# An FFN, attention and FFN layer on eight cores: other chunk split, residual update over two PSUM banks, final scale on one engine, weights cast by the DMA

## The reference

```
x += 1/2 swiglu(rmsnorm(x), w_ffn1_in, w_ffn1_out)      # (silu(g) * u) @ w_out
h  = rmsnorm(x);  q, k, v, forget gates = h @ w_in
o  = concat(8 forgetting-attention heads, 4 differential-attention heads)
x += o @ w_out
x += 1/2 swiglu(rmsnorm(x), w_ffn2_in, w_ffn2_out)
y  = rmsnorm(x)
outputs: y, new k, v and log forget gates, for prompt (2048 rows) and samples (4 x 32 rows a core)
```

## Time and profile before

| | |
|---|---|
| median of 3 runs | 1653.27 us (1652.67 to 1654.9) |
| profiled execution | 1653.27 us, span of its slowest core 1651.5 us |
| spans of the 8 cores | 1642.0 to 1651.5 us, granted TensorE clock 0.988 to 0.991 |
| PE / DVE / ACT / POOL busy | 95% / 44% / 42% / 15% of the span |
| chain that ended last | 83% PE, 5% issue, 4% ACT, 3% DVE, 2% DMA |
| DMA | 137.62 MB; POOL's queue 74.93 MB in 27.3% of 16 engines' span, SP's 60.51 MB in 10.6% |

### The profile page before, as it was taken

One profiled execution on the slowest core, in us unless ns is written; L12 is line 12 of the kernel. 1 busy time (PEld: TensorE's weight loads), 2 busy tenths in 40 slices (PEclk: granted clock), 3 DMA queues, 4 the chain that ended last, 5 costly groups with the idle time before them and its releaser, 6 DMA issues.

```text
span 1651.5 us, 34146 instructions; the slowest of 8 cores (1642.0 to 1651.5 us)
## 1 busy us (share of the span) xinstructions
PE 1562.6 (95%) x11654; PEld 856.6 (52%) x11654; DVE 727.8 (44%) x1489; ACT 690.0 (42%) x1402; POOL 246.1 (15%) x440
## 2 busy tenths in 40 slices
PE   5999999999997998999999999999999999999985
PEld 2544444444443576666766666544544444444431
DVE  4425224325236476666754444454234225234156
ACT  4510110110125576777789999964110110110134
POOL 3200000000013323232321121111000000000035
PEclk9999999999998999999999999999999999999998
DMA  9360131220217547656557555441620320320014
GB/s 288 81 108 14 28 62 21 44 40 14 52 28 207 167 96 135 129 114 125 104 114 138 119 121 121 90 129 52 117 37 0 71 39 1 59 38 2 13 56 161
DMA packets 41642, 137.62 MB, mean 83 GB/s; under 512 B 5121, under 2 KB 7809, under 8 KB 39810
## 3 DMA queue, kind: packets, MB, share of 16 engines
q0 software_dynamic: 17856, 74.93, 27.3%
q1 hardware_dynamic: 23618, 60.51, 10.6%
HBM read 174.63 MB, written 35.72 MB: 127 GB/s over the span
## 4 chain that ended last, share of the span: by engine, by line
PE 83%; issue 5%; ACT 4%; DVE 3%; DMA 2%; POOL 1%; SPq 0%; ACTq 0%; DVEq 0%; POOLq 0%
PE ps L161 82%; PE ps L171 1%; DMA xspill<-s_x 1%; DMA s_x<-xin 1%; DVE s_x L206 1%; DVE s_hn_68 L206 1%; ACT s_P_113 L190 1%; ACT s_junk L190 1%; DMA ko<-s_stage_93 1%; ACT s_P_117 L190 1%; ACT s_P_118 L190 1%; ACT s_P_114 L190 0%; ACT s_P_119 L190 0%; ACT s_P_115 L190 0%; ACT s_P_116 L190 0%
## 5 line engine op out<-in xcount | busy, mean ns | idle before, releaser
L206 DVE SCALAR_TENSOR_TENSOR s_x<-ps,s_x 128x512 f32<-128x512 f32 x272 | 186.7, 690 | 135.3 <-PE ps L161 135.2
L190 ACT ACTIVATE s_sg_91<-ps 128x512 f32<-128x512 f32 (+1 forms) x110 | 58.7, 533 | 430.9 <-PE ps L161 430.9
L190 ACT ACTIVATE s_sg_92<-ps 128x512 f32<-128x512 f32 (+1 forms) x110 | 58.7, 533 | 329.3 <-PE ps L161 328.5
L161 PE MATMUL ps<-s_wb_83,s_actT 128*128 128x512 bf16 x748 | 170.5, 385 | 15.6 <-DVE s_x L206 15.5
L161 PE MATMUL ps<-s_hT,s_wa_78 128*128 128x512 bf16 (+1 forms) x960 | 182.7, 351 | 0.9 <-DVE s_hT L206 0.9
L161 PE MATMUL ps<-s_hT,s_wa_79 128*128 128x512 bf16 (+1 forms) x960 | 179.7, 347 | 0.0
L206 DVE TENSOR_TENSOR s_actT<-s_sg_91,ps 128x512 bf16<-128x512 f32 (+1 forms) x110 | 66.9, 608 | 247.3 <-PE ps L161 242.5
L206 DVE TENSOR_TENSOR s_actT<-s_sg_92,ps 128x512 bf16<-128x512 f32 (+1 forms) x110 | 66.8, 608 | 247.2 <-PE ps L161 244.5
L161 PE MATMUL ps<-s_wb_82,s_actT 128*128 128x512 bf16 x748 | 164.7, 378 | 0.3 <-DVE s_x L206 0.3
L161 PE MATMUL ps<-s_hT,s_wa_81 128*128 128x512 bf16 (+1 forms) x800 | 149.7, 347 | 0.0
L161 PE MATMUL ps<-s_hT,s_wa_80 128*128 128x512 bf16 (+1 forms) x800 | 149.5, 347 | 0.0
(11 more groups left out here) (348 smaller groups left out, 2249.3 us busy)
## 6 DMA issues: line engine op xcount, KB each, us to landing
s_x<-xin SPq DMA_DIRECT2D x17, 512.0 KB, 21.4
xspill<-s_x SPq DMA_DIRECT2D x17, 512.0 KB, 3.1
y<-s_x SPq DMA_DIRECT2D x17, 512.0 KB, 2.8
s_Vc_87<-vc POOLq DMA_DIRECT2D x11, 520.0 KB, 7.2
s_Vc_88<-vc POOLq DMA_DIRECT2D x11, 520.0 KB, 7.1
s_kTc_84<-kTc POOLq DMA_DIRECT2D x11, 512.0 KB, 5.3
s_kTc_85<-kTc POOLq DMA_DIRECT2D x11, 512.0 KB, 5.6
s_Vc_89<-vc POOLq DMA_DIRECT2D x10, 520.0 KB, 7.3
```

Source lines behind the costliest of these rows:

```text
L161: fns.append(lambda e, a=(out, l, r), s=s0, t=s1: e.matmul(a[0], a[1], a[2], start=s, stop=t, skip_group_check=True))
L190: return self.add("act", st, pr, lambda e: e.activation(out, in_, func, **kw), reads, writes, cost, 220.0, after=after)
L206: return self.add(eng, st, pr, lambda e: getattr(e, method)(*args, **kw), reads, writes, cost, 180.0, after=after)
```

## The change

- FFN quarters have 5, 5, 6 and 6 chunks.
- Phase B writes a tile's two halves into two neighbouring banks, pairs 4, 5 and 6, 7 in turn (in FFN 1's last quarter pairs 4, 5 and 0, 1), and DVE adds all 1024 columns in one instruction. The very last tile of FFN 2 is still added in halves.
- The final scale is DVE's alone, for each tile in one instruction, for the last tile in two halves, whose stores go onto SP's and ACT's queues. The square has the factor 1/32 in it, so that POOL only adds.
- The first four weight chunks are loaded by POOL's queue, cast on the way; `wst`, the casts, the early Silu and the wait of the first `wb` load are gone, and `hT` is always copied by ACT. SP's queue brings only `x`.
- The planner takes 190 GB/s for every DMA queue.

```diff
-DMA_GBPS = {"sp": 330.0, "act": 330.0, "pool": 185.0}
+DMA_GBPS = 190.0
...
-QUARTERS = [(0, 6), (6, 6), (12, 5), (17, 5)]
+QUARTERS = [(0, 5), (5, 5), (10, 6), (16, 6)]
...
-    for k in ("x0", "w0", "x1", "x2", "x3", "w1", "w2", "x4", "x5", "w3") + tuple("x%d" % t for t in range(6, NT)):
...
+    for t in range(NT):
+        S.dma("sp", "x", 0, x[:, t, :], xin[t], 512 * K)
...
-    S.act("c", 0, junk[:, 0:1], nhalf[:, 0:1], AF.Silu)
+    for c in range(4):
+        wa_load(w1a, c)
     S.dma("pool", "w", 1, dm[:, :, :], dmask_d[:, :, :], 160 * K)
-    for c in range(4):
-        for h in range(2):
-            o, i = wa[c][:, 4 * h:4 * h + 4, :], wst[c][:, 4 * h:4 * h + 4, :]
...
-            S.dma("pool", "w", 1, wq_[:, 0:nq, :], wbd[:, c0:c0 + nq, :], nq * 512 * K,
-                  after=[after_b[0]] if qi == 0 else ())
+            S.dma("pool", "w", 1, wq_[:, 0:nq, :], wbd[:, c0:c0 + nq, :], nq * 512 * K)
...
+            pairs = (4, 0) if qi == 3 and not final else (4, 6)
             for t in range(NT):
+                b = pairs[nxt("pb", 2)]
+                po = psum[:, 512 * b:512 * b + 1024]
+                split = final and qi == 3 and t == NT - 1
                 for dh in range(2):
-                    po = PS[4 + nxt("pb", 2)]
...
+                if not split:
+                    xa = x[:, t, :]
                     S.dve("f", 10, "scalar_tensor_tensor", (xa, po[:, :], 0.5, xa, ALU.mult, ALU.add), [po[:, :], xa],
-                          [xa], 512)
+                          [xa], DM)
...
-        if t % 2 == 0 and t < NT - 1:
-            S.act("n2", 11, xt, xt, AF.Copy, scale=r)
-            S.dve("n2", 12, "tensor_tensor", (xt, xt, gt[:, :], ALU.mult), [xt, gt[:, :]], [xt], DM, eng="pool",
-                  rate=1.2)
...
+        halves = [slice(0, 512), slice(512, DM)] if t == NT - 1 else [slice(0, DM)]
+        for i, cs in enumerate(halves):
+            S.act("n", 12, junk[:, cs], x[:, t, cs], AF.Square, scale=1.0 / 32, accum=sp_[0][:, i:i + 1])
...
+        for i, cs in enumerate(halves):
+            xt = x[:, t, cs]
+            S.dve("n", 12, "scalar_tensor_tensor", (xt, xt, r, gt[:, cs], ALU.mult, ALU.mult), [xt, r, gt[:, cs]], [xt],
+                  DM // n)
+            S.dma(("sp", "act")[i], "y", 1, y_d[t, :, cs], xt, 512 * K // n)
```

More of the change, by code:

```diff
@@ L213, in dma @@
         return self.add(q, st, pr, lambda e: e.dma_start(out=out, in_=in_), reads, writes, cost,
-                        nbytes / DMA_GBPS[q], dma=True, after=after, dread=dread, dwrite=dwrite)
+                        nbytes / DMA_GBPS, dma=True, after=after, dread=dread, dwrite=dwrite)
     def schedule(self):
@@ L483, in build_nc @@
     grow = sb("grow", [1, DM], F32, 189 * K)
-    orow = sb("orow", [1, 128], F32, 185 * K)
-    wst = [sb("wst%d" % i, [128, 8, 256], F32, o * K) for i, o in enumerate((119, 127, 177, 193))]
+    orow = sb("orow", [1, 128], F32, 193 * K)
     lim = 68 * K
@@ L578, in build_nc, with norm_tile @@
     trb = [6, 7]
-    def norm_tile(t, pr, dve=False):
+    def norm_tile(t, pr):
         xt = x[:, t, :]
@@ L589, in norm_tile, with ffn @@
         S.tr("n", pr, [(PSB[b][:, k * 128:(k + 1) * 128], h[:, k * 128:(k + 1) * 128]) for k in range(8)], ident)
[L590 to L596, removed]
+        S.act("h", pr, hT[:, :, t * 128:(t + 1) * 128], PSB[b][:, :].rearrange("p (k c) -> p k c", k=8), AF.Copy)
+    def ffn(wad, wbd, after_silu, tile_done, first_norm, final=False):
         last = {"silu": None}
@@ L620, in phase_a @@
             S.dve("f", 10, "tensor_tensor", (a, s_, pu, ALU.mult), [s_, pu], [a], sn)
-        after_b = [None]
         for qi, (c0, nq) in enumerate(QUARTERS):
@@ L628, in ffn @@
                     phase_a(c, c, si)
-                    if si == 3 and after_b[0] is None:
-                        after_b[0] = last["silu"]
                 rest = range(4, nq)
@@ L639, in ffn @@
                     phase_a(c0 + cl, cl, si)
+            pairs = (4, 0) if qi == 3 and not final else (4, 6)
             for t in range(NT):
+                b = pairs[nxt("pb", 2)]
+                po = psum[:, 512 * b:512 * b + 1024]
+                split = final and qi == 3 and t == NT - 1
                 for dh in range(2):
-                    po = PS[4 + nxt("pb", 2)]
-                    S.mm("f", 20, [(po[:, :], actT[:, cl, t * 128:(t + 1) * 128], wq_[:, cl, dh * 512:(dh + 1) * 512],
-                                    cl == 0, cl == nq - 1) for cl in range(nq)])
-                    xa = x[:, t, dh * 512:(dh + 1) * 512]
+                    cs = slice(dh * 512, dh * 512 + 512)
+                    S.mm("f", 20, [(po[:, cs], actT[:, cl, t * 128:(t + 1) * 128], wq_[:, cl, cs], cl == 0, cl == nq - 1)
+                                   for cl in range(nq)])
+                    if split:
+                        xa = x[:, t, cs]
+                        S.dve("f", 10, "scalar_tensor_tensor", (xa, po[:, cs], 0.5, xa, ALU.mult, ALU.add),
+                              [po[:, cs], xa], [xa], 512)
+                if not split:
+                    xa = x[:, t, :]
                     S.dve("f", 10, "scalar_tensor_tensor", (xa, po[:, :], 0.5, xa, ALU.mult, ALU.add), [po[:, :], xa],
-                          [xa], 512)
+                          [xa], DM)
                 if qi == 3:
@@ L656, in done1 @@
         S.dma("sp", "x", 1, xs_d[t], x[:, t, :], 512 * K, dwrite=[("xs", t)])
[L658 to L663, removed]
+    silu1 = ffn(w1a, w1b, (), done1, lambda t: norm_tile(t, 5))
     def ld(q, dst, src, kb):
@@ L1175, in done2 @@
             S.dma("sp", "g", 0, gt[:, :], gvec_d[3:4, :].broadcast_to([128, DM]), 512 * K)
-        xt = x[:, t, :]
         sp_ = stat()
-        S.act("n", 12, junk[:, :], xt, AF.Square, accum=sp_[0][:, 0:1])
-        r = rstd_of("n", 12, sp_, 1.0 / DM)
-        if t % 2 == 0 and t < NT - 1:
-            S.act("n2", 11, xt, xt, AF.Copy, scale=r)
-            S.dve("n2", 12, "tensor_tensor", (xt, xt, gt[:, :], ALU.mult), [xt, gt[:, :]], [xt], DM, eng="pool",
-                  rate=1.2)
[L1184 to L1189, removed]
+        halves = [slice(0, 512), slice(512, DM)] if t == NT - 1 else [slice(0, DM)]
+        for i, cs in enumerate(halves):
+            S.act("n", 12, junk[:, cs], x[:, t, cs], AF.Square, scale=1.0 / 32, accum=sp_[0][:, i:i + 1])
+        n = len(halves)
+        ssap, r = sp_[0], sp_[1][:, 0:1]
+        S.dve("n", 12, "tensor_scalar", (r, ssap[:, 0:1], ssap[:, 1:2] if n == 2 else 0.0, EPS, ALU.add, ALU.add),
+              [ssap[:, 0:n]], [r], 1, eng="pool")
+        S.dve("n", 12, "tensor_tensor", (r, r, NHALF, ALU.pow), [r, NHALF], [r], 1, eng="pool", fixed=600.0)
+        for i, cs in enumerate(halves):
[3 more added lines that the diff above has]
+            S.dma(("sp", "act")[i], "y", 1, y_d[t, :, cs], xt, 512 * K // n)
+    ffn(w2a, w2b, le, done2, norm3, final=True)
     S.schedule()
```

## The result

The changed kernel takes 1633.98 us (median; 1633.07 to 1635.13) against 1653.68 us of the kernel before in the same comparison: a ratio of 0.9881, with a 95% interval of 0.9864 to 0.9898. It is 1.2% faster, and inside the range, but 9 us above the 1625 that was forecast.

The account below looks back on a forecast made before the run. TensorE was taken as busy nearly throughout, the largest single loss being 20.2 us in FFN 2's last phase B. Gains 19.2 + 2.9 + 1.7 + 0.7 + 3.5 = 28.0 from 1653.3 gave 1625 us, range 1614 to 1641.

Parts of the forecast that it names:

- (a): FFN 2's last phase B: VectorE scale, six chunks, wide update turn a 20.2 us loss into 1.0; 19.2 gained.
- (b): Five-chunk quarters: two-bank pairs let a 1.2 us update run during 2.16 us of PE work; 2.9 us gained.
- (c): Tail after PE's end: last tile in halves, first half's update under second half's matmuls; 1.7 us gained.
- (d): End of FFN 1: memset behind tile 3's rstd, PE gap 8.6 us instead of 10.8, projection waits; 0.7 gained.
- (e): Start: x tiles 4.4 us apart, PE continuous from 44 us against 47.43; 3.5 us gained.
- (f): Silu table load, FFN 2's first wb load and attention order: no cost, 0 us.
- Rival 2: Last phase: every POOL rstd step blocks DVE's scale, 3.3 us per tile; 1636 us, chance 0.12.
- Rival 1: Start: POOL-queue loads hold x tiles to 6.8 us each, continuous stretch from 51 to 52; 1632.5 us, chance 0.17.
- Rivals 3: Last phase: planner puts each scale before the next tile's update, VectorE's order is serial; 1667 us, chance 0.05.
- 4: Planner not better fed by 190 GB/s, attention stage reordered and 10 us worse; 1635 us, chance 0.06.

Follow-up runs that it names:

- experiment 3: Kernel before with only the final scale changed (VectorE alone, last tile in halves, second half's store on ScalarE's queue), old split and 512-wide updates: 1636.2 us.
- 4: Changed kernel with the old split of the chunks, 6,6,5,5 instead of 5,5,6,6, wide updates kept: 1640.4 us.
- experiments 2: Changed kernel with the planner's old DMA rates (330, 330 and 185 GB/s instead of 190 for all), the run with the 10.29 us gap: 1641.7 us.
- 6: Changed kernel with the first qz memset cut into four pieces behind the rstd of tiles 8 to 11, the run with the 5.72 us gap: 1631.2 us.
- the run with everything together: Changed kernel with first wb load held, both last stores on SP's queue, memset pieces and wfab's load late: 1613.75 us, ratio 0.9769 to the kernel before.

## Why the prediction was right or wrong

Gains by the table, of what was forecast:

| step | forecast | measured | from |
|---|---|---|---|
| (a), and (b) in FFN 2 | 19.2 + 1.9 | 22.0 | 507.9 - 485.9 |
| (b) in FFN 1 | 1.0 | 1.3 | 361.3 + 14.7 - 7.3 - 367.4 |
| (c) tail | 1.7 | 0.1 | 10.4 - 10.3 |
| (d) end of FFN 1 | 0.7 | 2.0 | 57.8 + 7.3 - 60.5, less 27.1 - 24.5 |
| (e) start | 3.5 | -6.7 | 124.8 - 14.7 - 116.8 |
| (f) attention, out projection | 0 | -0.7 | 511.2 + 48.9 - 511.7 - 49.1 |

Together that is 18.0 of 28.0; the time gained 19.7, as it is the slowest core's and the table has the median core.

- **(a) right.** No stall is left of the 20.2, so the 1.0 kept for one wasn't needed. Scale and split each carry a part: the scale alone 13.6 in FFN 2 and 0.8 in the tail, and without the split 5.8 is lost again. The wide update carries none here, as far as the runs show: with the old split, last phase and tail together are 52.8 without it (experiment 3) and 52.7 with it (4); its gain is that of (b). Rival 2 is out: every whole scale takes 1.28. But the rule of the Trainium skill that was weighed against this step (page "SBUF — State Buffer", section "Who interferes with whom") is not refuted by that: in all 16 whole tiles of this phase POOL's steps (0.23 and 0.56) run beside an update, which has one input in PSUM, and none beside a scale. Where one does meet such an instruction of DVE, at 514.87 in FFN 1, POOL's step takes 1.38 instead of 0.55 and DVE's stays at 1.29, and there the trace agrees with the rule. The prediction's have no such meeting either (POOL's steps end at 536.05, the scale begins at 536.16).
- **(b) right,** 36.7 us for five chunks, in FFN 1 as in FFN 2.
- **(c) failed in a place it didn't count, and was lucky before it.** From PE's end to the landing of the last store it is 7.6 us instead of 9.4, close to the 1.7 forecast. But only 1.1 of that is work, 5.2 instead of 6.3 up to the end of the last scale: the first half's update did not lie under the second half's matmuls, as DVE was still at tile 14's scale, and began at 1622.33, as PE ended. Another 0.7 is the landing of a store of half the size (2.3 instead of 3.0), which the sum did not have. What failed is the end of the program behind it: from that landing to the span's end SP's list takes 2.7 us instead of 1.0. With the store on SP's queue that is 1.2, and the tail 8.7, the forecast's figure.
- **(d) right in its mechanism:** the memset behind tile 3's rstd, and a projection that waits 1.5 us for DVE. The gap was 7.25, not 8.6. What it missed is that the gap costs more than its length: taking it away gave 10.2 us (60.5 - 50.3). On the core shown it is 10.6: 7.25, a second wait of 0.90, and some 2.4 that PE's clock costs. The stretch has 0.94 where that without a gap has 1.00; eight transposes behind the gap take 1.01 us (0.61 otherwise), 11 matmuls 3.61 (12 take 2.75). Behind the gaps of 10.29 and 5.72 us of experiments 2 and 6 the phase is 3.1 and 2.4 us longer than the gap alone makes it.
- **(e) wrong, by 10.2 us, which is the miss.** The step that failed is "when both queues are full, each moves 1.44 MB in 12 us, so an `x` tile takes 4.4 us". The earlier trace rows had 396 packets on each queue, and only because those were of one size did the bytes come out even. It held while `wa` was loaded (tiles about 5 us apart); under `wb` tile 7 took 10 us. The Trainium skill states the rule (page "DMA: Bandwidth & Descriptors", section "Queues, rings and completion order": an engine goes round the queues that have work, one packet each), and the trace agrees as far as its counts go, 86 packets against 86. POOL's queue also began sooner than read: its first load landed at 9.3 us, so `x` 3 landed at 19.6, not 15.5.
- **Rival 1, with a chance of 0.17, is what came about** (1632.5), in amount and place, though not by its mechanism: one hole of 10 us at tile 7, not 6.8 a tile. The measured time lies inside the range because the range took in this rival; it is above the 1617 to 1633 that the forecast gave itself. And a late tile cost that much because PE's order has its transposes ahead of 24 matmuls of the first block that do not need it: they stood ready behind it for 6.9 us.
- **Rivals 3 and 4 are out:** the next update comes before the scale, and the old rates are 7.7 us slower in the changed kernel. The rates matter at the start and the end of FFN 1, not in the attention (512.4 with the old ones), so (f) stands: the 0.7 lost there are less than the runs differ by (511.4 to 514.3).

## What to carry to other kernels

When two DMA queues are both full, reckon with equal packets, not equal bytes: look up the packet size of each load, and hold back a load with large packets until the small ones that the first matmuls need have landed. A wait on an in-order engine is worth its length plus what stands behind it, and on PE what the clock costs afterwards (2.4 to 3.1 us here), so look for the whole class (here, everything on GpSimd's queue that is to be written where a tile is still being stored) before moving one member of it away. If a planner writes the order, its rates and the transfers belong together: here either one changed alone was slower than both or neither.

## What the runs showed of the hardware

- Two full DMA queues moved the same number of packets, 86 and 86 in 6 us, and 0.88 against 0.29 MB.
- PE's granted clock behind a wait: 0.66 between 40 and 50 us in the changed kernel, where PE stood for 6.9 us, a mix of 1.2 and 2.4 GHz; eight matmuls behind the wait took 3.40 us, eight ahead of it 1.89. In the run with everything together, which has no wait there, it is 1.00. The stretch in the one and in the other:

```profile
40.00:50.00 10.00, 4.03 (x16) 2.03 (x17) 3.17 (x3) 6.85 (x11) 1.97 (x6) 0.66 1.01 336
```

```profile
40.00:50.00 10.00, 9.90 (x70) 5.33 (x69) 6.54 (x7) 8.63 (x15) 4.00 (x8) 1.00 0.49 170
```

- One 1024-wide update over two PSUM banks takes DVE 1.23 us, hardly less than two 512-wide ones (1.27). The five-chunk phases went from 37.7 and 38.6 to 36.7 with it; whether one hand-over instead of two or the two more banks did that, no run separates.
- A step of POOL that met a DVE instruction with two inputs in SBUF took 1.38 us instead of 0.55, and the DVE instruction 1.29, as elsewhere.
